# Pool's weight sums for the second side of the first half-step FFN: released by the first token half's operands instead of the second's

## The reference

```python
def swiglu(h, wg, wu, wd):
    return (jax.nn.silu(h @ wg) * (h @ wu)) @ wd

def ffn_half(x, g, wg, wu, wd):
    return x + 0.5 * swiglu(rms_norm(x, g), wg, wu, wd)
```

## Time and profile before

| | |
|---|---|
| median of 3 runs | 2379.29 us (2377.57 to 2381.19) |
| the profiled execution's own time | 2377.02 us |
| its span, first to last instruction | 2375.1 us |
| PE busy | 2321.7 us, 98% of the span |
| DVE, ACT, POOL busy | 66%, 38%, 30% |
| first group of the first half-step begins | 60.10 us |
| TensorE clock granted, mean over the span | 0.993 of full speed |

### The profile page before, as it was taken

How to read it: one execution, slowest core, us unless ns; L and a number is a source line. 1 busy time by engine, 2 the same in 40 slices (tenths; PEclk the granted TensorE clock), 3 DMA queues, 4 the chain that set the end, 5 groups by cost and what they waited for, 6 DMA issues and landing times. The chain is left out here.

```text
span 2375.1 us, 43001 instructions
## 1 busy us (share of the span) xinstructions
PE 2321.7 (98%) x17413; PEld 2270.5 (96%) x17413; DVE 1566.6 (66%) x2542; ACT 910.3 (38%) x1877; POOL 722.2 (30%) x631
## 2 busy tenths in 40 slices
PE   8999999999999999999899999999799999999998
PEld 5999999999999999999899999999799999999998
DVE  7888787875565554444455744467887878875554
ACT  6433434344452332233322222245533333434443
POOL 1566666630011111011100200023456566650000
PEclk9999999999999999999999999999899999999999
DMA  5544444486654332122433631134344444458663
GB/s 200 194 151 155 161 150 158 156 276 222 198 180 168 124 121 65 52 70 68 114 119 106 190 123 63 45 92 140 134 153 155 148 161 145 160 193 276 213 216 117
DMA packets 246790, 352.20 MB, mean 148 GB/s; under 512 B 12597, under 2 KB 179473, under 8 KB 245952
## 3 DMA queue, kind: packets, MB, share of 16 engines
q1 hardware_dynamic: 234288, 300.47, 39.0%
q0 software_dynamic: 12304, 48.98, 6.2%
HBM read 248.74 MB, written 100.66 MB: 147 GB/s over the span
## 5 line engine op out<-in xcount | busy, mean ns | idle before, releaser
L446 PE MATMUL ps<-uh,stream_high 128*128 128x352 f32 (+1 forms) x1392 | 456.2, 328 | 9.0 <-DVEq L3153 7.0
L447 PE MATMUL ps<-uh,stream_low 128*128 128x352 f32 (+1 forms) x1392 | 446.4, 321 | 0.0
L448 PE MATMUL ps<-ul,stream_high 128*128 128x352 f32 (+1 forms) x1392 | 444.7, 319 | 0.0
L888 PE MATMUL ps<-ffn_right_h,ffn_left_h 128*128 128x258 f32 x1144 | 323.6, 283 | 5.3 <-DVE outer L927 2.4
L890 PE MATMUL ps<-ffn_right_l,ffn_left_h 128*128 128x258 f32 x1144 | 322.8, 282 | 0.0
L889 PE MATMUL ps<-ffn_right_h,ffn_left_l 128*128 128x258 f32 x1144 | 322.6, 282 | 0.0
L446 PEld LDWEIGHTS ps<-uh,stream_high 128*128 128x128 f32 x1392 | 262.6, 189 | 18.3 <-issue 15.6
L447 PEld LDWEIGHTS ps<-uh,stream_low 128*128 128x128 f32 x1392 | 262.9, 189 | 0.8
L448 PEld LDWEIGHTS ps<-ul,stream_high 128*128 128x128 f32 x1392 | 262.5, 189 | 0.0
L1520 ACT ACTIVATE ffn_part<-ps 128x258 f32<-128x258 f32 x264 | 101.4, 384 | 382.0 <-PE ps L1491 306.5
L888 PEld LDWEIGHTS ps<-ffn_right_h,ffn_left_h 128*128 128x128 f32 x1144 | 216.4, 189 | 7.2 <-DVE ffn_right_l L917 6.5
(11 more groups left out here) (390 smaller groups left out, 6079.5 us busy)
## 6 DMA issues: line engine op xcount, KB each, us to landing
ffn_right_raw<-ffn_rows SPq DMA_DIRECT2D x143, 258.0 KB, 3.4
stream_raw<-in_w_in SPq DMA_DIRECT2D x25, 1024.0 KB, 5.4
ffn_rows<-ffn_hid SPq DMA_DIRECT2D x44, 516.0 KB, 5.2
stream_raw<-in_w_up SPq DMA_DIRECT2D x22, 1024.0 KB, 5.3
ffn_left_raw<-ffn_cols SPq DMA_DIRECT2D x88, 256.0 KB, 3.0
stream_raw<-in_w_gate SPq DMA_DIRECT2D x21, 1024.0 KB, 5.4
ffn_left_raw<-in_w_down SPq DMA_DIRECT2D x55, 256.0 KB, 2.8
ffn_rows<-x SPq DMA_DIRECT2D x22, 516.0 KB, 4.5
```

The costliest lines, as they stand in the source:

```text
L446: pe.matmul(out, w_high, a_high, start=first, stop=False)
L447: pe.matmul(out, w_low, a_high, start=False, stop=False)
L448: return pe.matmul(out, w_high, a_low, start=False, stop=last)
L888: pe.matmul(out, w_h, a_h, start=opens and p == 0, stop=False, skip_group_check=True)
```

## The change

Pool's wait ahead of the sums of side 1 asks for the low parts of one token half instead of both, in the half-step that has no `entry`; the second half-step keeps its count. Each engine has the same instructions in the same order as before; what changes is one number that one wait compares with.

```diff
             for q in range(SIDES):
                 if q == 0:
-                    gp.wait_ge(rights.low_done, 2 * ALL)
+                    gp.wait_ge(rights.low_done, 2 * ALL if entry else ALL)
                 if q + 1 < SIDES:
                     lefts.gpsimd(gp, q + 1)
                 if q % 2 == 0:
```

## The result

The changed kernel takes 2383.67 us (median of 16 runs, 2380.46 to 2387.87), the kernel before 2379.04 beside it: ratio 1.0018, 95% interval 1.0011 to 1.0024. That is 4.6 us slower; forecast was 4.4, from 2379.29 to 2383.7. The forecast total was right by luck in part: two of its terms were off, and their errors made up for each other.

What follows compares the result with a forecast made beforehand. PE, busy 98% of the span, bounds the kernel, with DVE setting the pace of this stretch. 4.05 - 1.62 = +2.4, plus 2.0 for the clock, gives +4.4 us on 2379.29: 2383.7 us, range 2380.0 to 2387.0.

Steps and rivals of the forecast that it cites:

- The start of the sums: Pool, side 1: the four sums begin about 64.2 instead of 73.46, 9.3 us earlier.
- The loss on DVE: DVE from 61.35 to past 73.29: four sums and the first gate delay its instruction of 73.29 by 4.05 us.
- the term 4.05: DVE's delay before group 1's stall: 3.87 us for four sums plus 0.18 for the gate; bounds 3.5 and 4.95.
- the signs named ahead: Pool sums near 2.2 us, line 549 over 2 us, one PE stall near 5 us, slow clock, line 696 mostly 0.68.
- The price of one turn: Each Pool sum between two large DVE instructions delays DVE by 2.23 - 1.15 = 1.08 us.
- One stall of 5.05 us: PE, group 1, before its third product: the stall of 1.00 us becomes 5.05 us (73.58 to 78.63).
- The second stall: PE, group 2, before its third product: the 1.62 us lost there goes, as DVE gains 3.1 us.
- Rival C: Gates, not sums, make DVE late at 84 us, so the second stall stays: +6.1 to +7.1 us; chance 0.15.
- The clock: Behind the long PE stall, part of the time at the 1.2 GHz level: +2.0 us, bounds 1.7 and 3.1.
- Rival B: The 4.05 and 1.62 hold but the clock stays up: +2.4 us, 2381.7; chance 0.17.
- The theory: Pool's early sums hold up DVE, DVE holds up ACT and PE, the second stall goes, the clock takes more.
- rival D: Pool does not get in between DVE's back-to-back instructions; sums use DVE's gaps: 0 to -2.6 us; chance 0.10.

Runs made afterwards that it cites:

- the sums behind the third difference: Changed kernel with one more Pool wait ahead of the early sums, for the third difference of the second token half (line 553); ratio 1.0022, 5.1 us over the kernel before.
- the second profile: The changed kernel run and profiled once more with no edit; ratio 1.0018, 4.4 us over the kernel before.
- The fills at the old place: Kernel before with side 1's four sums replaced by zero fills of the same tiles at their old place; ratio 0.9993, 1.6 us below the kernel before.
- the fills: Changed kernel with the four early sums replaced by zero fills of the same tiles; ratio 0.9996, 1.7 us below the kernel before.

## Why the prediction was right, and where it was not

**The start of the sums: right.** 63.41 is 4.01 us after line 536; forecast was 64.2 - 60.09 = 4.11.

**The loss on DVE: too small.** The step that failed is the term 4.05, with its upper bound of 4.95, made up turn by turn from the earlier trace rows. Measured is 5.29 and 5.32, because one instruction lost three turns in a row: 5.28 - 1.23 = 4.05 there and 2.31 - 1.23 = 1.08 on the next. Four sums got in ahead of DVE, as forecast; but the first three cost 4.05 where the prediction had 1.08 + 0.96 + 0.75 = 2.79, because they came in one piece and none lay beside a take. So of the signs named ahead, sums near 2.2 us and low parts (line 549) over 2 us did not come. The price of one turn (1.08) was right, and where turns are taken (the sums behind the third difference) the loss is 3.74. What the prediction lacked is a row for sums queued behind transfers beside a DVE that is already at work; in the earlier trace rows the DVE instruction begins while a sum runs.

**One stall of 5.05 us: wrong in shape.** DVE lost its time before a rounding that a copy of group 0 waits behind, so PE stalled there too: 2.09 and then 3.80 us, and 2.07 and 2.30 us in the second profile, 4.4 us together. The 1.31 us ahead of them in the first profile come from PE's early start of group 0 and not from the change. Neither sum is the cost; what sets the end is when the wait of group 1 ends, 5.29 us later after line 536 (79.18 - 59.40 against 74.58 - 60.09).

**The second stall goes, 1.62 us: right.** Lines 696 and 1617 take 5.34 - 7 x 0.68 = 0.58 and 2.14 - 4 x 0.42 = 0.46 us over their time alone, 1.04 left; forecast was 1.0. The fills at the old place show that it was the sums and not the gates. Rival C is refuted.

**The clock, +2.0 with bounds 1.7 and 3.1: mis-sized, and not one number.** It fell in both profiles of the changed kernel, behind different stalls. In the first it cost 5.1 - (5.29 - 1.62) = 1.4 us, in the second nothing, because it fell and rose again while PE was ahead of DVE; in other runs up to 2.5, by the same subtraction. The bounds should have begun at zero: the earlier trace rows show how long the clock stayed low, not what that cost by the end of PE's next wait. Rival B has the cost right in the second profile, though not its reason: the clock fell there too.

**The sum.** 5.3 - 1.6 + 0 to 1.4 gives +3.7 to +5.1; the median moved by 4.6, where 4.05 - 1.62 + 2.0 = 4.4 stood. DVE's loss came out 1.2 us over the forecast and the clock 0.6 to 2.0 us under it; that the two cancelled is luck. The theory, that Pool's reads hold up DVE, is shown by the fills; rival D (DVE keeps its turn) is refuted, the opposite came.

## What to carry to other kernels

A wait that looks idle on one engine may be what keeps it off a resource that a busier engine needs: before releasing work earlier, price it on the engine that it may hold up, not on the one that waited. A stall that is set by another engine's lateness is measured by when it ends, not by how long it is; the same stall was 2.30, 3.80 or 0.41 us with the same end. And where an in-order engine has a short release for someone else queued behind an instruction that waits, moving the release ahead takes the stall away and leaves the wait as it is: here PE came 1.7 us earlier at its mark, as much as with the sums taken away (1.5).

## What the runs showed of the hardware

A DVE instruction that reads two tiles of SBUF waits for sums of Pool that read SBUF, not for fills of Pool that only write it: 5.28 against 1.23 us from the same start. So two engines can also hold each other up where no semaphore stands between them. The Trainium skill says that such a DVE instruction contends with Pool instructions that read SBUF and not with those that only write it ("SBUF — State Buffer", "Who interferes with whom"), and the runs agree. The same section of the Trainium skill holds that whichever issues first gets the shared ports for its whole instruction. A trace shows starts, not issues, and the profile calls its spans on Pool rough; by the recorded starts it fits the sums behind the third difference (DVE 64.11, sum 64.34, DVE first), but not the changed kernel: the DVE instruction of 63.08 began before the sum of 63.41 and came after it and two more, both times and in every run with the same queue, and with a fill between it began 0.80 us before the first sum.

The granted clock fell to its 1.2 GHz level behind an idle time of 2.07 us (70.84 in the second profile) and stayed full in the kernel before behind 1.46 us. But it also stayed full behind 2.09 us at the same place of the first profile (1.00 in 72 to 76 us), so the length of one stall does not tell. The same kernel had it at one place in one execution and at another in the next, and the cost went from 1.4 us to nothing.
